# Two transformer blocks in float32 on one core: stationary weights read from every second column

## The reference, cut to what matters

```python
proj = x @ w_in                                   # 1024 -> 7680, split in ten parts
merged = g0 * (ya @ w_branch[0]) + g1 * (yb @ w_branch[1]) + g2 * (yc @ w_branch[2])
h = merged @ w_mix_out
q = (x @ xa_q); k, v = split(mem @ xa_kv)         # cross-attention, then @ xa_o
u, gt = split(x @ ffn_w_in); h = (silu(dwconv(gt) + b) * u) @ ffn_w_out
```

## Time and profile before

| | |
|---|---|
| median of three runs | 1636.41 us |
| span of the profiled execution (first to last instruction) | 1634.2 us |
| TensorE matmul busy | 1620.2 us, 13,642 instructions |
| TensorE weight load busy | 1584.0 us, 13,642 instructions |
| VectorE busy | 1155.2 us |
| ScalarE busy | 868.8 us |
| bytes read from HBM | 300.52 MB, 188 GB/s over the span |

### The profile page before, as it was taken

How to read it: one execution, slowest core, us unless ns; L and a number is a source line. 1 busy time by engine, 2 the same in 40 slices (tenths; PEclk the granted TensorE clock), 3 DMA queues, 4 the chain that set the end, 5 groups by cost and what they waited for, 6 DMA issues and landing times.

```text
span 1634.2 us, 32191 instructions
## 1 busy us (share of the span) xinstructions
PE 1620.2 (99%) x13642; PEld 1584.0 (97%) x13642; DVE 1155.2 (71%) x1730; ACT 868.8 (53%) x1305; POOL 40.5 (2%) x59
## 2 busy tenths in 40 slices
PE   9999999999999999999999999999999999999998
PEld 9999999999999999999999999999999999999998
DVE  6588778658666767977974866568576545877777
ACT  5456544646444454555355644455755555464554
POOL 3030000000000000000000000000000000000000
PEclk9999999999999999999999999999999999999999
DMA  9984456535656564445564465655454453556562
GB/s 313 305 213 155 149 197 248 194 130 187 209 173 206 168 238 168 161 149 188 201 234 160 151 227 178 207 173 186 163 173 168 155 180 132 192 168 207 173 204 102
DMA packets 83071, 305.85 MB, mean 187 GB/s; under 512 B 10704, under 2 KB 10832, under 8 KB 80752
## 3 DMA queue, kind: packets, MB, share of 16 engines
q1 hardware_dynamic: 77280, 279.44, 50.1%
q0 software_dynamic: 5648, 24.35, 5.0%
HBM read 300.52 MB, written 6.29 MB: 188 GB/s over the span
## 4 chain that ended last, share of the span: by engine, by line
PE 90%; DVE 7%; issue 1%; ACT 1%; DMA 0%; SPq 0%; DVEq 0%; ACTq 0%
PE general L621 56%; PE general L625 14%; PE scores L663 5%; PE attention_out L663 3%; PE probs_transposed L663 3%; DVE weights_lo L1622 2%; PE attention_out L815 2%; PE scores L748 1%; PE probs_transposed L767 1%; PE scores L839 1%; ACT weights_hi L1166 1%; DVE x_tok L1696 1%; DVE x_tok L1693 1%; DVE xT_lo_part L1632 1%; PE attention_out L859 1%
## 5 line engine op out<-in xcount | busy, mean ns | idle before, releaser
L1622 DVE TENSOR_TENSOR weights_lo<-raw_weights,weights_hi 128x1024 fp32r<-128x1024 f32 x525 | 633.4, 1222 | 372.0 <-ACT weights_hi L1166 369.4
L1166 ACT ACTIVATE weights_hi<-raw_weights 128x1024 fp32r<-128x1024 f32 x525 | 553.2, 1058 | 390.6 <-PE general L621 219.0
L621 PE MATMUL general<-xT_hi_part,weights_hi 128*128 128x256 f32 x2432 | 683.4, 281 | 2.3 <-DVE weights_lo L1622 2.0
L621 PE MATMUL general<-xT_lo_part,weights_hi 128*128 128x256 f32 x2432 | 674.8, 277 | 0.0
L621 PE MATMUL general<-xT_hi_part,weights_lo 128*128 128x256 f32 x2432 | 674.7, 277 | 0.0
L621 PEld LDWEIGHTS general<-xT_hi_part,weights_hi 128*128 128x128 f32 x2432 | 457.4, 188 | 10.5 <-issue 8.8
L621 PEld LDWEIGHTS general<-xT_lo_part,weights_hi 128*128 128x128 f32 x2432 | 457.2, 188 | 1.4 <-issue 1.0
L621 PEld LDWEIGHTS general<-xT_hi_part,weights_lo 128*128 128x128 f32 x2432 | 458.0, 188 | 0.0
L1965 DVE SCALAR_TENSOR_TENSOR exp_ring<-general,param_cols,exp_ring 128x255 f32<-128x255 f32 (+1 forms) x176 | 76.8, 478 | 46.2 <-ACT exp_ring L1362 44.7
L1362 ACT ACTIVATE exp_ring<-general,param_cols 128x256 f32<-128x256 f32 x88 | 44.9, 561 | 69.6 <-PE general L621 69.6
L625 PE MATMUL general<-weights_hi,xT_hi_part 128*128 128x256 f32 x272 | 76.6, 281 | 0.0
(11 more groups left out here) (328 smaller groups left out, 2947.4 us busy)
## 6 DMA issues: line engine op xcount, KB each, us to landing
raw_weights<-in_stream SPq DMA_DIRECT2D x525, 512.0 KB, 4.2
attention_area<-in_ln_rows POOLq DMA_DIRECT2D x9, 1024.0 KB, 5.2
bias_scratch<-in_rpb POOLq DMA_DIRECT2D x32, 96.0 KB, 10.5
attention_area<-bias_scratch POOLq DMA_DIRECT2D x2, 1536.0 KB, 8.9
memT_hi<-memT_scratch POOLq DMA_DIRECT2D x2, 1024.0 KB, 5.0
memT_lo<-memT_scratch POOLq DMA_DIRECT2D x2, 1024.0 KB, 8.8
attention_area<-in_mem SPq DMA_DIRECT2D x2, 512.0 KB, 6.0
z_tok<-in_x SPq DMA_DIRECT2D x1, 1024.0 KB, 10.5
```

The source lines that it names most:

```text
L621: ins = nc.tensor.matmul(ps[b][0:m, half * T:half * T + T], w[wk][:, half * m:half * m + m], x[xk_], start=first, stop=last, skip_group_ch ...
L1166: nc.scalar.activation(hi_half(h), raw_half(h), ACT.Copy).then_inc(*hi_done.more())
L1622: nc.vector.tensor_tensor(lo_half(h), raw_half(h), hi_half(h).bitcast(F32), ALU.subtract).then_inc(*lo_done.more())
```

## The change

The host lays out the tiles of every feature-major block so that the two 128-column slices alternate: number 2j of a row is column j, number 2j+1 is column 128+j (`woven`, `held_tiles`). TensorE then reads its stationary operand with a step of two numbers (8 bytes), starting at 0 or at 1. The values that each matmul holds, the instructions, their order, their number and the tiles' places are the same as before. For `uq` the 768 columns are padded by head (8 x 96 to 8 x 128) where they were padded by pair of heads (4 x 192 to 4 x 256), so that the step-two read finds the same 96 columns of each head. Tiles of blocks with the activation held (values, `xa_o`, `w_mix_out`, `w_o_2`, the second product of the feed-forward part) keep their layout. The laying out is done on the host and is not part of the time.

```diff
--- before.py
+++ after.py
@@ -619,7 +619,7 @@
                             last = kc == kcs - 1 and half == 1 and n == 2
                             if feature_major:
                                 ins = nc.tensor.matmul(ps[b][0:m, half * T:half * T + T],
-                                                       w[wk][:, half * m:half * m + m], x[xk_], start=first, stop=last,
+                                                       w[wk][:, half:half + 2 * m - 1:2], x[xk_], start=first, stop=last,
                                                        skip_group_check=True)
                             else:
                                 ins = nc.tensor.matmul(ps[b][:, half * T:half * T + T],
@@ -2374,6 +2374,16 @@
     return w.reshape(k // P, P, -1, TILE_N).transpose(2, 0, 1, 3).reshape(-1, P, TILE_N)
 
 
+def woven(tiles):
+
+    return tiles.reshape(-1, P, 2, P).transpose(0, 1, 3, 2).reshape(-1, P, TILE_N)
+
+
+def held_tiles(w):
+
+    return woven(tiles_of(w))
+
+
 def halves_of(tiles):
 
     t = np.concatenate(tiles)
@@ -2382,33 +2392,36 @@
 
 def stream_of(i):
 
-    keys = [tiles_of(i["xa_kv"][l][:, :D]).reshape(4, DC, P, TILE_N) for l in range(DEPTH)]
+    keys = [held_tiles(i["xa_kv"][l][:, :D]).reshape(4, DC, P, TILE_N) for l in range(DEPTH)]
     memory = tiles_of(i["w_mem_kv_2"][0]).reshape(4, DC, P, TILE_N)
+    memory_keys = woven(memory[0:2]).reshape(2, DC, P, TILE_N)
     t = list(keys[0])
     for l in range(DEPTH):
         w = i["w_in"][l]
         cuts = {n: w[:, 512 * k:512 * k + 512]
                 for k, n in enumerate(("qa", "ka", "va", "qn", "kn", "vn", "gb", "gc", "hc"))}
-        t += [tiles_of(cuts[n]) for n in ("qa", "ka", "va", "qn", "gc", "hc", "gb", "kn", "vn")]
-        t.append(tiles_of(w[:, 4608:]))
+        t += [(tiles_of if n in ("va", "vn") else held_tiles)(cuts[n])
+              for n in ("qa", "ka", "va", "qn", "gc", "hc", "gb", "kn", "vn")]
+        t.append(held_tiles(w[:, 4608:]))
         t += branch_tiles(i["w_branch"][l], (0, 2, 1))
         t.append(tiles_of(i["w_mix_out"][l]))
-        q = tiles_of(i["xa_q"][l]).reshape(4, DC, P, TILE_N)
+        q = held_tiles(i["xa_q"][l]).reshape(4, DC, P, TILE_N)
         v = tiles_of(i["xa_kv"][l][:, D:]).reshape(4, DC, P, TILE_N)
         t += [v[0], v[1], q[0], q[1], q[2], v[2], q[3], v[3], tiles_of(i["xa_o"][l])]
         ffn = ffn_tiles(i["ffn_w_in"][l], i["ffn_w_out"][l], True)
         if l + 1 < DEPTH:
             t += [keys[l + 1][0], keys[l + 1][1]] + ffn + [keys[l + 1][2], keys[l + 1][3]]
         else:
-            t += [memory[0], memory[1]] + ffn + [memory[2], memory[3]]
+            t += [memory_keys[0], memory_keys[1]] + ffn + [memory[2], memory[3]]
     w = i["w_in_2"][0]
-    uq = i["w_uq_2"][0].reshape(384, 4, 192)
-    uq = np.concatenate([uq, np.zeros((384, 4, 64), uq.dtype)], 2).reshape(384, 1024)
+    uq = i["w_uq_2"][0].reshape(384, 8, 96)
+    uq = np.concatenate([uq, np.zeros((384, 8, 32), uq.dtype)], 2).reshape(384, 1024)
     ukv = i["w_ukv_2"][0].reshape(256, 8, 128)
-    g = tiles_of(w[:, 5792:]).reshape(12, DC, P, TILE_N)
-    dq, dk, dv = (tiles_of(w[:, 672 + 1536 * k:672 + 1536 * (k + 1)]).reshape(6, DC, P, TILE_N) for k in range(3))
-    t += [tiles_of(w[:, 0:672]), tiles_of(w[:, 5280:5792]), g[4], g[5], g[6], tiles_of(uq),
-          tiles_of(ukv[:, :, :64].reshape(256, 512)), tiles_of(ukv[:, :, 64:].reshape(256, 512)), g[7]]
+    g = held_tiles(w[:, 5792:]).reshape(12, DC, P, TILE_N)
+    dq, dk, dv = (lay(w[:, 672 + 1536 * k:672 + 1536 * (k + 1)]).reshape(6, DC, P, TILE_N)
+                  for k, lay in enumerate((held_tiles, held_tiles, tiles_of)))
+    t += [tiles_of(w[:, 0:672]), held_tiles(w[:, 5280:5792]), g[4], g[5], g[6], held_tiles(uq),
+          held_tiles(ukv[:, :, :64].reshape(256, 512)), tiles_of(ukv[:, :, 64:].reshape(256, 512)), g[7]]
     t += list(dq) + list(dk) + [dv[0], dv[2], dv[4], dv[1], dv[3], dv[5], g[8], g[9], g[10], g[11]]
     t += [g[0], g[1], g[2], g[3]]
     t += branch_tiles(np.stack([i["w_br_mla_2"][0], i["w_br_dil_2"][0], i["w_br_mem_2"][0]]), (0, 1, 2))
@@ -2419,13 +2432,13 @@
 
 def branch_tiles(w, order):
 
-    parts = [tiles_of(x).reshape(4, 4, P, TILE_N) for x in w]
+    parts = [held_tiles(x).reshape(4, 4, P, TILE_N) for x in w]
     return [parts[br][cb] for cb in range(4) for br in order]
 
 
 def ffn_tiles(w_in, w_out, gate_last):
 
-    a, b = tiles_of(w_in[:, :FF]), tiles_of(w_in[:, FF:])
+    a, b = held_tiles(w_in[:, :FF]), held_tiles(w_in[:, FF:])
     gate, value = (b, a) if gate_last else (a, b)
     gate, value = gate.reshape(FPAIR, DC, P, TILE_N), value.reshape(FPAIR, DC, P, TILE_N)
     down = w_out.reshape(FC, P, D // TILE_N, TILE_N).transpose(0, 2, 1, 3).reshape(FPAIR, -1, P, TILE_N)
```

## The result

The change made the kernel slower: 1676.49 us (median; 1675.77 to 1677.34) against 1636.43 us (1634.76 to 1637.41) of the kernel before beside it, a ratio of 1.0245 with a 95% interval of [1.0232, 1.0257], some 40 us. The forecast was 1598.8 us, the range ended at 1664 us. The profiled execution after has a span of 1675.4 us, 41.2 us longer than the 1634.2 us of before.

A forecast was written before the change was run, and what follows sets the result against it. TensorE's matmul pitch was taken as the bound: 8736 x (114.6 - 110.3) = 37.6 us off at L621 turns 1634.2 into 1596.6 us, plus 2.2 us around the span gives 1598.8 us. The range was 1586 to 1664 us (0.80).

The forecast's parts named there:

- What bounds the kernel: Whole kernel: TensorE, busy 1620.2 of 1634.2 us, sets the time through the pitch of its matmuls; its waits are small.
- The load by itself: unchanged, about 107 ns: Weight loads at L621: a step of 8 bytes keeps a 128-column load at about 107 ns; 214 if columns cost two fetches.
- The 3 ns that the prediction put between two loads: Load chain at L621: 3 ns between loads plus 107 ns of loading gives the forecast pitch of 110.3 ns.
- The load beside the matmul: meeting costs, equal speeds heal it: L621: load and stream disturb each other in SBUF; walking at equal speeds lowers the mean pitch from 114.6 to 110.3 ns.
- The 6.7 ns of the low level: L621's 113.3 ns pitch over 106.7 ns of streaming: a surcharge expected to fall toward 2.4 ns if meeting is what costs.
- the 2.4 ns of the plain float32 products: Plain float32 matmuls: 215.7 ns, 2.4 over two passes of 106.7, read as the small surcharge of reads at equal speeds.
- low level only: Rival for L621: the step ends the 117.8 ns pitch but 113.3 ns stays; 1625.0 us, chance 0.20.
- More lines per load: Rival for L621: loads touching 1024 bytes collide more, pitch 117.8 ns throughout, 28.0 us more, 1664.4 us; chance 0.22.
- Two fetches a column: Rival for L621: the load takes 214 ns and becomes the bound, 895 us more, about 2531 us; chance 0.09.
- No difference: Rival for L621: the two pitches come from how a block is entered, not from addresses; 1636.4 us, chance 0.13.
- The 192 ns load of the earlier trace: First projections: load of `weights_lo` takes 192 ns, its neighbour 188, read as stream and load disturbing each other in SBUF.
- Other lines: Matmuls with the activation held (L625, L663, L955): they keep contiguous loads and get nothing.

The follow-up runs named there:

- m1: Bench of matmuls alone, step of the held load varied: 113.3 ns at step 1, 120.0 at step 2; with 128 columns streamed, 111.7 and 117.8 ns.
- m2: Bench of matmuls alone, streamed activation moved 0 to 256 bytes on: 113.3 to 119.9 ns with contiguous loads, 120.0 to 121.7 ns at step 2.
- m3: Bench of matmuls alone, streamed columns, stream grouping and load step varied: with 32 columns held, 256 streamed columns take 113.3 ns, 512 take 231.7 ns.
- k3b: Kernel before the change, with only the down product's held activation 128 bytes further on: 1637.52 us against 1635.61, ratio 1.0014.
- m5b: Bench of matmuls alone, one load in 3, 6 or 12 at step 2: 120.0, 116.65, 114.9 ns; also the held activation moved: 113.4 to 120.0 ns.
- k5c: Kernel before the change, with only 111 weight tiles woven and read at step two (666 strided loads): 1633.49 us against 1635.87, ratio 0.9986.
- k6: Kernel before the change, with the down product's activation 128 bytes on and 86 tiles woven (516 strided loads): 1624.29 us against 1635.81, ratio 0.993.

## Why the prediction was wrong

**What bounds the kernel** held: the span grew by what TensorE's pitches grew, 46.3 us of it at L621, and no wait took part.

**"The load by itself: unchanged, about 107 ns"** is the step that failed. Its bounds, 107 and 214 ns, held the truth, but the value taken, because the load's time had gone with the number of columns, was read from contiguous loads only the earlier trace rows. These take 4 columns from a line, and 32 lines at 1.77 ns lie far under 107. With two columns a line the 64 lines, 113.3 ns, come out over the columns, and the load of 128 columns took 117.8 ns from one to the next where nothing else could bound it (m1), 120.0 in the kernel. The 3 ns that the prediction put between two loads were too few as well: for contiguous loads they are 111.7 - 106.7 = 5.0 (m1), so that even with the load unchanged the chain came to 111.7 and not to 110.3. The Trainium skill ("SBUF — State Buffer", Door 1, the note on cachelines) asks for two accesses in a line for full bandwidth. By that rule the load would have kept its time; in these runs two are nearly enough (120.0 against 113.3), 4/3 are not (173.3), and one is half as fast (235.6).

**"The load beside the matmul: meeting costs, equal speeds heal it"** failed too. There is a cost of meeting, worth 0 to 6.6 ns by the place of the operands (m2), but contiguous loads of 128 columns at the kernel's own place, at the low level, show none of it. The 6.7 ns of the low level, which were to fall toward 2.4, are the stream's own 64 lines (m3, with 32 columns held). For the 2.4 ns of the plain float32 products the lines offer a reason without equal speeds: they need twice the cycles for the same lines, 215.7 ns for lines worth 113.3. That fits, and no run tested it. The low level was thus a floor for a change to the load (no series with 256 float32 columns streamed ran below 113.3 ns, whatever it held), and 1625.0 us, the bound of "low level only", was the best that it could bring. The term was sized at -4.3 ns a matmul and came out at +5.3.

**The rivals.** "More lines per load" named the right quantity, at 0.22, and had the right sign, but took the high level, 117.8 ns, as the most that lines can cost, since no row showed a third level; with 120.0 in its place it gives 1636.4 + 8736 x 5.4 = 1683.6 us, and the unforeseen fall of L663, 6.0 us, brings that to 1677.6, beside the 1676.5 measured; that these agree so well is partly luck, since L625's 3.2 us more and the shorter gaps' 3.3 us less are left out and cancel. The stated range ended with this rival's 1664.4. The row that spoke against it, that a quarter fewer columns did not lower the pitch, spoke for the stream as the bound, and so for there being nothing to gain. "Two fetches a column", 214 ns and more, is what a step of 4 costs (235.6 ns), not a step of 2. "No difference" fell with the first row after.

**The 192 ns load of the earlier trace rows** was read as a collision that a step would avoid. In the kernel it goes with the high level: the down products of before, whose loads are contiguous and whose stream is another, have it too (`ffn_act_hi` under `weights_lo`, median 192 ns), and after the change, at the low level, they have 188.

**Other lines** were costed at nothing. L663 gave 6.0 us and L625 took 3.2, with no instruction of theirs changed: the level depends on what ran before them, as k3b and m5b show for the down product; for L625 it was not followed.

## What to carry to other kernels

Count the 16-byte lines of both TensorE operands, not only their columns: for float32 reads here a line took 1.77 ns, so a pair of stream and load takes at least the longest of streamed columns, streamed lines, held columns and held lines. What comes on top, up to 9 ns here, is not foretold by that: it goes with the distance of the operands, with how many columns are held and with what ran before. One longer load costs its neighbours too. Before an operand's layout is changed, run the one instruction pair alone with the new address pattern: the bench's series at step 2 gave the kernel's 120.0 ns. Where two levels of one pitch appear in a trace, look at them block by block in order of time; here setting them by hand was worth 0.7%.

## What the runs showed of the hardware

- The 256-column float32 stream's 113.3 ns are 64 lines; over 192 to 512 columns a line took 1.77 to 1.85 ns. The price of a line in a load is the same at 2.4 and at 1.2 GHz (113.4 ns for 64 lines at the lower).
- Low and high level, 113.3 and 117.8 ns, are two states of the same instructions at the same addresses. A few strided loads at the start of a feature-major block set the state low (166 of 167 blocks in k5c and k6); a change of which operand is held can flip it, by the operand's distance.
- One strided load in six or twelve costs 19 to 20 ns, three times its own surplus, and in a run of only strided loads 6.7 each. Why a lone one costs its neighbours so much was not settled, nor what the 3.3 to 8.9 ns over a load's lines are, nor why 96 woven or 64 contiguous columns held run near 119 ns, nor why bfloat16 loads with one column a line ran at 109.2 ns.
